# A two-block transformer kernel: prefetches and side-by-side sums between stages, a shorter VectorE tail, four store places

## The chip, the cores and the metric

One core of a Trainium2 chip runs the whole program in one launch. The metric is device time in microseconds (us). The kernel before took 3588.96 us in the median of three runs (3581.26 to 3589.14).

## The reference, cut to what matters

A sequence of 1024 tokens of width 1024 goes through two blocks, all in float32.

```
# block 1
u = rms_norm(x); proj = u @ w_in
xa = causal_conv(x_rnn); r, i = sigmoid(xa @ wa + ba), sigmoid(xa @ wx + bx)
a = exp(-8 r softplus(-lam)); b = sqrt(1 - a*a) * (i * xa); h_t = a_t h_(t-1) + b_t
ya = h * gelu(g_rnn)
yb = attention(low-rank q, low-rank k and v, per-head rms_norm, rope)
x = x + (sigmoid(g0) * ya + sigmoid(g1) * yb) @ w_out
x = x + moe(rms_norm(x))      # 32 experts, top 2 in one group
# block 2
mix = [hgrn2(x) | multiscale_pool(x)] @ w_out_2
h = layer_norm(alpha * x + mix)
out = layer_norm(alpha * h + moe_2(h) + shared(h))   # 64 experts, top 8
```

Each expert is `(silu(x @ w_gate[e]) * (x @ w_up[e])) @ w_down[e]`, with weights of 3 MB.

## The kernel before, in words

The program is a chain of stages, one function each, and each has its own block of instruction streams. When a stage ends, its semaphores are cleared and all engines meet (`phase`, the `clear` callback), so that no engine enters the next stage before every engine, SyncE (SP) and GpSimd (POOL) among them, has finished this one. The order is: `begin` (norm and turn), `lru` (recurrence of block 1), `mla_project`, `attention`, `merge`, `route1`, `dispatch`, `experts`, `take_sums`, `hgrn`, `pooling`, `mix_out`, `route2`, `dispatch`, `experts`, `final_norm`. Within a stage each engine runs its own list in program order and waits on semaphores. SP issues nearly all loads and stores; they are served in order of issue.

`lru` works in four blocks of 256 channels. For each, TensorE (PE) does three groups of input products and two gate groups, ScalarE (ACT) takes each group out of PSUM with its function, and VectorE (DVE) does the convolution and then the tail: `hh = aa*aa` (L525), `pp` (L528), `ii*xa` (L531), `ii*pp` (L534), two scans (L537), `hh*gelu` (L539), `hh*gate` (L541). After block 4 PE also does the low-rank products of token tile 0 (`low_rank`, L571). POOL clears the second copy of the rows in which experts' outputs are summed (`zero_second`, L276).

`mla_project` goes over eight tiles of 128 tokens. PE turns the tile's low-rank rows (`turn_low`, L662), does the low-rank products of the next tile (`low_groups`, L653), then the up-projections (`up_groups`, L679), and between the query and the key/value part turns the heads of the tile before (`turn_heads`, L692, eight steps). ACT copies every turned group into `stage` (`take_heads`, L762); SP stores two steps together (L637) from one of two places of `stage`, so the fifth step waits until the store of the first two has landed.

`merge` computes the two sigmoid gates' remaining half with weights `w_gate` loaded at its start (L1102), then the output product. `route1` picks experts and has SP load the weights of the first five experts (L1626, L1631). `dispatch` works out which token stands in which slot and stores the weights per token (`dense`, L1454). `experts` loops over blocks of 2 x 64 slots: POOL gathers token rows (`gather`: L1753, L1756, L1757), PE turns them (L1814), DVE copies them out (L1911 for the first block, L1902 later) and also copies the second half's weights (`stage_gate_up`, L1888), PE multiplies (L1825, L1828, L1851, L1854), POOL adds the result to `token_sums` in DRAM (L1778). The two halves of a block go to two copies of the sums.

`take_sums` adds the two copies: SP loads tile t of the first (L1247), POOL then has a DMA add the second to it (`add_second`, L1230), PE turns it (L1260), DVE copies it (L1267). `final_norm` does the same addition and then the last layer norm and the stores. `pooling` loads its weights `w`, `w_pool` and `w_out` (L2287 to L2289) while POOL clears the second copy of the sums again.

Of the kernel before, what the change touches and what calls it, by code (L numbers as in the profile page):

```python
# [18 lines left out]
F32 = mybir.dt.float32  # L19
# [253 lines left out]
def zero_second(pool, sum_d, zero, zero_out):  # L273

    for t in range(T + 1):
        pool.dma_start(sum_d[S + P + t * P:S + P + (t + 1) * P, :], zero).then_inc(zero_out, 16)  # L276


def lru(nc, A, G, spare, sum_d, wcol, wgate, w_low, ps):
# [9 lines left out]
    with ph.ctx:  # L289
# [43 lines left out]
        def _(pool):  # L333
# [6 lines left out]
            zero_second(pool, sum_d, zero[:, 0:D], zero_out)  # L340
            pool.wait_ge(zero_out, 16 * (len(spare) + T + 1))
# [48 lines left out]
        def _(a):  # L390
# [9 lines left out]
            with a.Fori(0, NBLK // 2) as j:  # L400
                for u in range(2):
# [12 lines left out]
                    for k, (out, bias) in enumerate(((rr, vec(G, "lru_ba")), (ii, vec(G, "lru_bx")))):  # L414
                        a.wait_ge(group_ready, first + 4 + k)
# [7 lines left out]
                    a.wait_ge(log_ready, b + 1)  # L423

                    s.activation(pp[:], rr[:], ACT.Tanh, scale=-1.0).then_inc(p_ready, 1)
# [5 lines left out]
        def _(v):  # L431
# [66 lines left out]
            with v.Fori(0, NBLK) as b:  # L498
# [3 lines left out]
                for k in range(CONV):  # L502
                    for c in range(B):
# [10 lines left out]
                        else:  # L514
# [3 lines left out]
                d.memset(xp[:, :, 0:CONV - 1], 0.0).then_inc(pad_ready, 1)  # L518
                v.wait_ge(group_taken, 1 + b * GROUPS + 4)
# [3 lines left out]
                                ALU.mult).then_inc(log_ready, 1)  # L523
                v.wait_ge(act, b * 3 + 3)
# [5 lines left out]
                v.wait_ge(group_taken, 1 + b * GROUPS + 5)  # L530
                st(d.tensor_tensor(ii[:], ii[:], xa[:], ALU.mult))  # L531
                st.join()
# [5 lines left out]
                st.join()  # L538
                st(d.tensor_tensor(hh[:], hh[:], gelu[:], ALU.mult))  # L539
# [36 lines left out]
def mla_project(nc, A, G, qk_d, v_d, w_low, ps):  # L576
# [12 lines left out]
    with ph.ctx:  # L589
# [9 lines left out]
        stage = ph.sb("stage", [QK, 2, 2 * TURN, P])  # L599
# [3 lines left out]
        sq_low = ph.sb("sq_low", [P, Q_LORA + KV_LORA])  # L603
        rot_all = ph.sb("rot_all", [P, 4, HEADS, H2])
        rot = [rot_all[:, i] for i in range(4)]
        acc = ps[:, 0].rearrange("p b s -> p (b s)").rearrange("p (k n) -> p k n", n=BANK)
# [4 lines left out]
         st_out1, dve, act) = ph.sems(  # L611
            "w_in1 w_in2 acc_ready acc_taken row_sq row_ms row_rt row_ok tr_ready tr_taken "
            "q_sq qk_sq qk_ms qk_rt qk_ok ht_ready ht_taken v_out st_out0 st_out1 dve act")
        st_out = [st_out0, st_out1]
# [13 lines left out]
        def _(sp):  # L628
            sp.dma_start(w_uq[:], A["w_uq"].rearrange("l (c p) n -> p (l c) n", p=P)).then_inc(w_in1, 16)
            sp.dma_start(w_ukv[:], A["w_ukv"].rearrange("l (c p) n -> p (l c) n", p=P)).then_inc(w_in2, 16)  # L630
            for t in range(T):
                sp.wait_ge(acc_taken, number["up", t, NQ + NKV - 1] + 1)
                sp.dma_start(v_d[t * P:(t + 1) * P, :], vv[:].rearrange("p h d -> p (h d)")).then_inc(v_out, 16)
                for n in range(TURNS // 2):
# [3 lines left out]
                                 stage[:, n % 2]).then_inc(st_out[n % 2], 16)  # L638
            sp.wait_ge(v_out, 16 * T)
            for q in st_out:  # L640
                sp.wait_ge(q, 16 * T * TURNS // 4)

        @block.tensor
        def _(pe):
# [60 lines left out]
        def _(a):  # L705
# [49 lines left out]
            def take_heads(t):  # L755
                for n in range(TURNS):
                    m = t * TURNS + n
                    a.wait_ge(ht_ready, m + 1)
                    d = (m // 2)
                    if n % 2 == 0 and d >= 2:  # L760
                        a.wait_ge(st_out[(n // 2) % 2], 16 * (d // 2))
                    s.activation(stage[:, (n // 2) % 2, (n % 2) * TURN:(n % 2 + 1) * TURN, :],  # L762
# [80 lines left out]
def attention(nc, A, G, qk_d, v_d, mask_d):  # L843
# [25 lines left out]
    with ph.ctx:  # L869
# [42 lines left out]
        def _(sp):  # L912
# [20 lines left out]
            for p in range(PAIRS - 2):  # L933
                reload(p)

# [125 lines left out]
def merge(nc, A, G, rows_d, sum_d, logits):  # L1061
# [5 lines left out]
    COL = 2 * D + Q_LORA + KV_LORA + ROPE + D  # L1067
    HC = C // 2
    with ph.ctx:
        w_gate = ph.sb("w_gate", [P, 2, C, D // 4])  # L1070
# [17 lines left out]
        (wg0, wg1, wo_in, x_in, g_ready, g_taken, m_ready, o_ready, o_taken, dve) = ph.sems(  # L1088
            "wg0 wg1 wo_in x_in g_ready g_taken m_ready o_ready o_taken dve")
        wg = [wg0, wg1]  # L1090
# [5 lines left out]
        def _(sp):  # L1096
            w = A["w_in"].rearrange("l (c p) n -> p (l c) n", p=P)
            for q in range(Q):
                if q >= 2:
                    sp.wait_ge(g_ready, (q - 1) * PERQ)  # L1100
                c0 = COL + q * (D // Q)
# [132 lines left out]
def take_sums(nc, G, sum_d, rows, cols):  # L1234

    ph = phase(nc)
    with ph.ctx:
# [11 lines left out]
        @block.gpsimd  # L1249
        def _(pool):  # L1250
            add_second(pool, sum_d, rows, row_in, both_in)
# [1472 lines left out]
```

## Time and profile before

| | us |
|---|---|
| median of 3 runs | 3588.96 |
| the profiled execution | 3588.82 |
| its span in the profile | 3587.1 |
| PE busy | 3219.0 (90%) |
| DVE busy | 1568.1 (44%) |
| ACT busy | 727.7 (20%) |
| POOL busy | 729.1 (20%) |

PE is busy for nine tenths of the span; the other tenth lies mostly between stages. A view of waits lists who waited for whom; a row of the timeline gives start, duration, engine and line, what is written from what, and in brackets the idle time before it and what ended it. A name such as `second` can stand for several tensors in turn, since the kernel uses two large buffers again and again.

### The profile page before, as it was taken

The page shows a single profiled execution, that of the slowest core. Times are in us where ns is not written, and L with a number is a line of the kernel's source. Part 1 is how long each engine was busy: PE and PEld are TensorE (multiplying, and loading weights), DVE is VectorE, ACT ScalarE, POOL GpSimd, SP SyncE. Part 2 cuts the span into 40 slices and gives each one's busy share as a digit, 9 for nine tenths or more (in the row PEclk, how much of TensorE's full clock was granted, in tenths as well). Part 3 has the DMA queues.
Part 4 walks back from the last instruction along what each step waited for, and adds up shares of the span by engine and source line. Part 5 has one row for each costly group of instructions (what it writes and reads, how often), then busy time and mean ns, then how long its engine had stood idle before and what let it go on. Part 6 is the DMA issues. An engine that isn't in the chain of part 4 may idle for free. (4 is left out here: it accounts for less than half of the span.)

```text
span 3587.1 us, 44543 instructions
## 1 busy us (share of the span) xinstructions
PE 3219.0 (90%) x14147; PEld 1604.3 (45%) x14148; DVE 1568.1 (44%) x2350; ACT 727.7 (20%) x1169; POOL 729.1 (20%) x932
## 2 busy tenths in 40 slices
PE   8999899978998995989779996989799999999992
PEld 4444455545664454333257773455333333333330
DVE  3332224455773123434336773334344444444444
ACT  2222123334552011011023230121011111111112
POOL 1000000000000000444410000000255555555552
PEclk9999999998999996999879998989899999999996
DMA  6110021123212115899541003111698999988876
GB/s 221 41 41 29 0 100 49 51 56 83 72 48 83 66 71 208 306 382 384 186 118 34 25 1 126 68 58 58 241 307 266 330 323 313 297 278 274 275 245 182
DMA packets 177205, 564.82 MB, mean 157 GB/s; under 512 B 18636, under 2 KB 88880, under 8 KB 139952
## 3 DMA queue, kind: packets, MB, share of 16 engines
q1 hardware_dynamic: 139456, 428.64, 31.5%
q0 software_dynamic: 35856, 133.74, 15.2%
q10 hardware_dynamic: 1800, 1.20, 0.1%
q8 instruction: 58, 0.95, 0.1%
q14 instruction: 35, 0.29, 0.0%
HBM read 460.27 MB, written 103.27 MB: 157 GB/s over the span
## 5 line engine op out<-in xcount | busy, mean ns | idle before, releaser
L1825 PE MATMUL gu_ps<-w_gu,second 128*64 x1680 | 755.5, 603 | 13.2 <-DVE h L1888 8.0
L1828 PE MATMUL gu_ps<-h,second 128*64 128x512 f32 x1680 | 755.5, 603 | 0.0
L1825 PEld LDWEIGHTS gu_ps<-w_gu,second 128*64 128x64 f32 x1680 | 224.3, 138 | 456.0 <-issue 444.1
L1753 POOL COPY idx<-moe_slot_tok 128x1 int32 (+1 forms) x109 | 22.2, 204 | 1782.4 <-POOLq L95 1739.9
L1851 PE MATMUL y_ps<-w_dn,hid_t 128*64 x824 | 375.6, 598 | 2.5 <-issue 2.2
L1854 PE MATMUL y_ps<-second,hid_t 128*64 128x512 f32 x824 | 375.6, 598 | 0.0
L352 PE MATMUL front<-second,wcol 128*128 128x512 f32 x768 | 330.4, 592 | 4.8 <-ACTq L63 2.4
L1888 DVE COPY h<-w_gu 128x4096 f32 x109 | 249.5, 2290 | 71.6 <-SPq L1705 71.3
L352 PEld LDWEIGHTS front<-second,wcol 128*128 128x128 f32 x768 | 145.8, 190 | 188.6 <-issue 188.6
L1773 POOL TENSOR_TENSOR idx_y<-moe_slot_tok,moe_side 128x1 int32<-128x1 int32 x103 | 123.4, 1198 | 522.3 <-ACT second L1874 522.3
L1828 PEld LDWEIGHTS gu_ps<-h,second 128*64 128x64 f32 x1680 | 224.3, 138 | 0.0
L1874 ACT ACTIVATE second<-y_ps,share 128x1024 f32<-128x1024 f32 x103 | 114.7, 1113 | 459.1 <-PE y_ps L1854 459.1
L1868 ACT ACTIVATE act_g<-gu_ps 128x256 f32<-128x256 f32 x105 | 40.3, 384 | 749.8 <-PE gu_ps L1828 749.8
L1851 PEld LDWEIGHTS y_ps<-w_dn,hid_t 128*64 128x64 f32 x824 | 104.3, 136 | 191.6 <-issue 180.0
L1777 POOL TENSOR_TENSOR mark_y<-tok 128x1 f32<-128x1 f32 x103 | 181.2, 1759 | 19.1 <-DMA token_sums<-second,idx_y 8.4
L1778 POOL DMA_INDIRECT token_sums<-second,idx_y x103 | 175.0, 1699 | 18.3 <-issue 17.4
L1900 DVE TENSOR_TENSOR hid<-act_g,gu_ps 128x256 f32<-128x256 f32 x105 | 44.2, 421 | 291.5 <-ACT act_g L1868 291.5
L1904 DVE COPY hid_t<-h_ps 128x256 f32<-128x256 f32 x105 | 44.5, 424 | 279.4 <-PE h_ps L1837 279.4
L1814 PEld LDWEIGHTS x_ps<-ident,xb 128*128 128x128 f32 x856 | 105.0, 195 | 108.6 <-issue 73.8
L1895 DVE COPY second<-w_dn 128x2048 f32 x105 | 129.0, 1229 | 47.1 <-issue 47.0
L1814 PE MATMUL x_ps<-ident,xb 128*128 128x128 f32 x856 | 125.8, 290 | 22.2 <-DMA xb<-token_rows,idx 21.9
L1902 DVE COPY second<-x_ps 128x1024 f32<-128x1024 f32 x105 | 128.5, 1224 | 24.5 <-PE x_ps L1814 24.5
(435 smaller groups left out, 4887.1 us busy)
## 6 DMA issues: line engine op xcount, KB each, us to landing
w_gu<-in_w_gate_dram SPq DMA_DIRECT2D x96, 1024.0 KB, 13.3
w_gu<-in_w_up_dram SPq DMA_DIRECT2D x96, 1024.0 KB, 17.3
w_dn<-in_w_down_dram SPq DMA_DIRECT2D x96, 1024.0 KB, 10.4
wcol<-in_w_in_dram SPq DMA_DIRECT2D x12, 1024.0 KB, 5.3
qk_by_head<-stage SPq DMA_DIRECT2D x32, 384.0 KB, 3.3
qk<-qk_by_head SPq DMA_DIRECT2D x16, 768.0 KB
token_sums<-zero POOLq DMA_DIRECT2D x19, 512.0 KB, 13.1
token_sums<-second SPq DMA_DIRECT2D x16, 512.0 KB, 2.6
```

Of the source, the lines that this page charges most:

```text
L352: last = nc.tensor.matmul(ps[:, slot, c, h * BANK:(h + 1) * BANK], wcol[:, k, kc, c * P:(c + 1) * P], G.u[:, kc, h * BANK:(h + 1) * BANK], ...
L1773: g.tensor_tensor(idx_y[:, slot:slot + 1], G.slot_tok[:, bass.ds(b, 1)], G.side, ALU.add).then_inc(idx_y_ready, 1)
L1777: g.tensor_tensor(mark_y[:, slot:slot + 1], G.tok[:, 0:1], G.tok[:, 0:1], ALU.add).then_inc(idx_y_ready, 1)
L1778: g.indirect_dma_start(sum_d, bass.IndirectOffsetOnAxis(ap=idx_y[:, slot:slot + 1], axis=0), y[:, slot, :], None, compute_op=ALU.add).then ...
L1814: last = nc.tensor.transpose(x_ps[:, c, :], xb[:, slot, c:D:C], G.ident[:])
L1825: nc.tensor.matmul(gu_ps[0:PART, slot], x_t[:, slot, c, 0:PART], w_gu[:, bass.ds(ws, 1), :, c, :].rearrange("p o g n -> p (o g) n"), start ...
L1828: last = nc.tensor.matmul(gu_ps[PART:P, slot], x_t[:, slot, c, PART:P], st_gu[:, slot, :, c, :], start=c == 0, stop=c == C - 1)
L1851: nc.tensor.matmul(y_ps[0:PART, cs], hid_t[:, slot, c, 0:PART], w_dn[:, bass.ds(ws, 1), c, cs].rearrange("p o n -> p (o n)"), start=c == 0 ...
L1854: last = nc.tensor.matmul(y_ps[PART:P, cs], hid_t[:, slot, c, PART:P], st_dn[:, c, cs], start=c == 0, stop=c == FC - 1)
L1888: d.tensor_copy(st_gu[:, slot].rearrange("p g c n -> p (g c n)"), w_gu[:, bass.ds(e % W, 1)].rearrange("p o g c n -> p (o g c n)")).then_i ...
L1895: d.tensor_copy(st_dn.rearrange("p c n -> p (c n)"), w_dn[:, bass.ds(e % W, 1)].rearrange("p o c n -> p (o c n)")).then_inc(d_staged, 1)
L1902: d.tensor_copy(x_t[:, 1 - slot], x_ps[:]).then_inc(x_ready, 1)
```

## The change

- `lru`, DVE: `gate*gelu` is done as soon as the gate has been taken, so one multiplication follows the scans in place of two; `ii*xa` goes ahead of `aa*aa`. ACT: `Tanh` goes between the two gate sigmoids.
- `lru`, POOL: after the first block it clears a third copy of the sums; the second expert loop and `final_norm` use that third copy, and `pooling` no longer clears anything.
- `mla_project`: `stage` has four places; `rot_all` and `sq_low` lie inside `sq`; for tile 0 `low_groups(1)` goes ahead of `turn_low(0)`.
- `attention`/`merge`: the first two parts of `w_gate` are loaded at the end of `attention`'s SP list.
- `route1` loads two experts; the other three are loaded at the head of `dispatch`'s SP list.
- `dispatch`: POOL gathers the rows of the first two blocks there (waiting for the slots and for the store of `dense`); some tiles of the first `dispatch` lie in the free large buffer. `experts` starts without these gathers, and DVE stages the weights of block 0 ahead of the copy of its rows.
- `take_sums`: ACT's queue loads the second copy by plain loads, DVE adds. `final_norm`: the same for the first two of eight tiles, the other six as before.

```diff
@@ lru
+            pool.wait_ge(block_done, 2)
+            zero_second(pool, sum_d, 2, zero[:, 0:D], zero_out)
...
+                        if k == 1:
+                            a.wait_ge(log_ready, b + 1)
+                            s.activation(pp[:], rr[:], ACT.Tanh, scale=-1.0).then_inc(p_ready, 1)
...
+                v.wait_ge(group_taken, 1 + b * GROUPS + 3)
+                st(d.tensor_tensor(gate[:], gate[:], gelu[:], ALU.mult))
...
+                v.wait_ge(group_taken, 1 + b * GROUPS + 5)
+                v.wait_ge(act, b * 3 + 2)
+                st(d.tensor_tensor(ii[:], ii[:], xa[:], ALU.mult))
                 v.wait_ge(act, b * 3 + 3)
                 st(d.tensor_tensor(hh[:], aa[:], aa[:], ALU.mult))
...
-                st(d.tensor_tensor(hh[:], hh[:], gelu[:], ALU.mult))
@@ mla_project
-        stage = ph.sb("stage", [QK, 2, 2 * TURN, P])
+        stage = ph.sb("stage", [QK, 4, 2 * TURN, P])
...
+                if t == 0:
+                    low_groups(1)
                 turn_low(t)
-                if t + 1 < T:
+                if 0 < t < T - 1:
                     low_groups(t + 1)
...
-                    if n % 2 == 0 and d >= 2:
-                        a.wait_ge(st_out[(n // 2) % 2], 16 * (d // 2))
+                    if n % 2 == 0 and t:
+                        a.wait_ge(st_out[n // 2], 16 * t)
@@ attention, sync
+            for q in range(2):
+                load_gate(sp, A, G, w_gate, q)
@@ take_sums
+        @block.scalar
+        def _(a):
+            for t in range(T):
+                at = S + P + t * P
+                a.dma_start(other[:, t, :], sum_d[at:at + P, :]).then_inc(row_in[t], 16)
...
+            for t in range(T):
+                v.wait_ge(row_in[t], 32)
+                d.tensor_tensor(rows[:, t, :], rows[:, t, :], other[:, t, :], ALU.add).then_inc(added, 1)
+                if t:
+                    take(t - 1)
+            take(T - 1)
@@ route1, sync
-            for e in range(W1):
+            for e in range(W_EARLY):
                 load_expert(sp, G, e, e)
@@ dispatch
+            if scores is None:
+                for e in range(W_EARLY, W1):
+                    load_expert(sp, G, e, e)
             sp.wait_ge(dense_ready, 1)
...
+        @block.gpsimd
+        def _(pool):
+            g = nc.gpsimd
+            pool.wait_ge(slots_ready, 1)
+            for b in range(2):
+                g.tensor_copy(G.idx[:, b:b + 1], G.slot_tok[:, b:b + 1]).then_inc(idx_ready, 1)
+            pool.wait_ge(idx_ready, 2)
+            pool.wait_ge(dense_out, 16)
+            g.tensor_tensor(G.mark[:], G.tok[:, 0:2], G.tok[:, 0:2], ALU.add).then_inc(idx_ready, 1)
+            for b in range(2):
+                g.indirect_dma_start(G.xb[:, b, :], None, rows_d, bass.IndirectOffsetOnAxis(
+                    ap=G.idx[:, b:b + 1], axis=0)).then_inc(G.xb_in[b], 16)
@@ experts
-            gather(0, 0)
-            gather(1, 1)
...
+            stage_gate_up(0, 0)
             v.wait_ge(x_turned, 1)
             d.tensor_copy(x_t[:, 0], x_ps[:]).then_inc(x_ready, 1)
-            stage_gate_up(0, 0)
             stage_gate_up(1, 1)
@@ pooling
-            nc.gpsimd.memset(zero[:], 0.0).then_inc(cleared, 1)
-            pool.wait_ge(cleared, 1)
-            zero_second(pool, sum_d, zero[:], zero_out)
-            pool.wait_ge(zero_out, 16 * (T + 1))
@@ final_norm (FIRST = 2)
+            for t in range(FIRST):
+                at = 2 * (S + P) + t * P
+                a.dma_start(other[:, t, :], sum_d[at:at + P, :]).then_inc(other_in[t], 16)
...
+            for t in range(FIRST):
+                v.wait_ge(row_in[t], 16)
+                v.wait_ge(other_in[t], 16)
+                d.tensor_tensor(G.h[:, t, :], G.h[:, t, :], other[:, t, :], ALU.add).then_inc(both_in[t], 1)
```

## Rows read from the trace of the kernel before

**Rows 1.** The page, part 1: busy us, share, instructions.

```profile
PE 3219.0 (90%) x14147; PEld 1604.3 (45%) x14148; DVE 1568.1 (44%) x2350; ACT 727.7 (20%) x1169; POOL 729.1 (20%) x932
```

**Rows 2.** Waits of PE, whole run: us in total, times, longest us.

```profile
PE tp L1260 <- DMA second<-token_sums: 35.7, 8, 29.6
...
PE x_ps L1814 <- DMA xb<-token_rows,idx: 21.9, 2, 15.0
PE u_ps L2310 <- DMA w_pool<-in_w_pool_dram: 19.9, 1, 19.9
PE front L692 <- ACT stage L762: 17.9, 22, 2.1
...
PE front L662 <- DVE low L798: 16.8, 1, 16.8
...
PE ps L1133 <- DMA w_gate<-in_w_in_dram: 8.3, 1, 8.3
```

**Rows 3.** Timeline, end of the first recurrent stage.

```profile
423.85 1.91 ACT L425 ACTIVATE pp<-rr 128x2048 f32<-128x2048 f32 x1
...
433.54 2.28 DVE L531 TENSOR_TENSOR ii<-ii,xa 128x2048 f32<-128x2048 f32 x1
...
445.13 2.29 DVE L541 TENSOR_TENSOR h<-hh,gate 128x2048 f32 x1
```

**Rows 4.** Timeline, start of the projection stage.

```profile
448.24 0.17 DVE L786 COPY gains<-vec 128x6 f32<-128x6 f32 x1 [0.82 <-PEq L95]
...
452.72 1.97 PE L662 MATMUL front<-ident,low 128*128 128x128 f32 x8 [16.82 <-DVE low L798]
...
469.41 15.61 PE L679 MATMUL front<-w_uq,low_t 128*128 128x512 f32 x36
```

**Rows 5.** DMA issues: line, count, KB each, median us to landing.

```profile
w_ukv<-in_w_ukv_dram SPq DMA_DIRECT2D x1, 2048.0 KB, 18.3
...
w_pool<-in_w_pool_dram SPq DMA_DIRECT2D x1, 256.0 KB, 17.2
...
token_rows<-dense SPq DMA_DIRECT2D x1, 128.0 KB, 21.5
```

**Rows 6.** Timeline, heads turned in tile 6 of the projection stage.

```profile
747.02 1.05 PE L692 MATMUL front<-ident,qk 128*96 128x128 f32 x8 [0.28 <-ACT stage L762]
...
750.14 1.13 PE L692 MATMUL front<-ident,qk 128*96 128x128 f32 x8 [2.07 <-ACT stage L762]
```

**Rows 7.** Timeline, start of the merge stage.

```profile
1117.28 1.02 SPq L1102 DMA_DIRECT2D w_gate<-in_w_in_dram  x2
...
1123.81 11.53 PE L1133 MATMUL ps<-second,w_gate 128*128 128x512 f32 x21 [8.35 <-DMA w_gate<-in_w_in_dram]
```

**Rows 8.** Timeline, first dispatch and start of the first expert loop.

```profile
1404.14 0.38 SPq L1454 DMA_DIRECT2D token_rows<-dense  x1
...
1430.44 1.05 POOL L1757 DMA_INDIRECT xb<-token_rows,idx  x1 [0.37 <-issue]
...
1434.90 1.98 PE L1814 MATMUL x_ps<-ident,xb 128*128 128x128 f32 x8 [6.94 <-DMA xb<-token_rows,idx]
```

**Rows 9.** Timeline, the stage that adds the two copies of the sums.

```profile
1788.67 4.16 SPq L1247 DMA_DIRECT2D second<-token_sums  x8
...
1822.23 1.09 PE L1260 MATMUL tp<-ident,second 128*128 128x128 f32 x8 [0.66 <-DMA second<-token_sums]
1823.36 1.22 DVE L1267 COPY h<-tp 128x1024 f32<-128x1024 f32 x1 [0.53 <-PE tp L1260]
```

**Rows 10.** One window of that stage: length, busy us, PEclk, DMA share, GB/s.

```profile
1791.00:1792.00 1.00, 0.00 (x0) 0.00 (x0) 0.00 (x0) 0.00 (x0) 0.00 (x0) 0.50 1.01 385
```

**Rows 11.** Timeline, start of the second expert loop.

```profile
2533.47 0.49 SPq L1631 DMA_DIRECT2D w_dn<-in_w_down_dram  x1
...
2540.80 1.97 PE L1814 MATMUL x_ps<-ident,xb 128*128 128x128 f32 x8 [14.97 <-DMA xb<-token_rows,idx]
```

**Rows 12.** Groups by line: busy us, mean ns, idle before.

```profile
L1888 DVE COPY h<-w_gu 128x4096 f32 x109 | 249.5, 2290 | 71.6 <-SPq L1705 71.3 <-issue 0.2
```

More of the change, by code:

```diff
@@ L840, in _, with attention @@
             norm_heads(T - 1)
-def attention(nc, A, G, qk_d, v_d, mask_d):
+def attention(nc, A, G, qk_d, v_d, mask_d, w_gate):
     ph = phase(nc)
@@ L1237, in take_sums @@
     with ph.ctx:
+        other = ph.sb("other", [P, T, D])
         tp = ph.ps("tp", [P, 2, C, P])
-        turned, taken = ph.sems("turned taken")
+        turned, taken, added = ph.sems("turned taken added")
         row_in = ph.sems(" ".join(f"row_in{t}" for t in range(T)))
-        both_in = ph.sems(" ".join(f"both_in{t}" for t in range(T)))
         block = ph.ctx.enter_context(nc.Block())
@@ L1255, in _ @@
             for t in range(T):
-                pe.wait_ge(both_in[t], 16)
+                pe.wait_ge(added, t + 1)
                 if t >= 2:
@@ L1406, in shared_add, with dispatch, room @@
                                    op0=ALU.mult, op1=ALU.add).then_inc(G.sh_added, 1)
-def dispatch(nc, G, K, E, NB, rows_d, sum_d, scores=None):
+def dispatch(nc, G, K, E, NB, rows_d, sum_d, n, scores=None):
     ph = phase(nc)
     with ph.ctx:
-        m = ph.sb("m", [P, T, E])[:] if scores is None else G.m
-        before = ph.sb("before", [P, T + 1, E])
-        dense = ph.sb("dense", [P, T, E])
+        taken = [0]
+        def room(name, n):
+            if scores is not None:
+                return ph.sb(name, [P, n])[:]
+            taken[0] += n
+            return G.u[:].rearrange("p c s -> p (c s)")[:, taken[0] - n:taken[0]]
+        m = room("m", T * E).rearrange("p (t e) -> p t e", e=E) if scores is None else G.m
+        before = room("before", (T + 1) * E).rearrange("p (t e) -> p t e", e=E)
+        dense = room("dense", T * E).rearrange("p (t e) -> p t e", e=E)
         cnt = ph.sb("cnt", [P, E])
@@ L1658, in experts @@
         w_gu, w_dn = G.w_gu, G.w_dn
-        idx = ph.sb("idx", [P, 2], I32)
         idx_y = ph.sb("idx_y", [P, 2], I32)
-        mark = ph.sb("mark", [P, 2])
         mark_y = ph.sb("mark_y", [P, 2])
@@ L1664, in experts @@
         share_b = ph.sb("share_b", [P, 2])
-        xb = ph.sb("xb", [P, 2, D + E])
+        xb, idx, mark = G.xb, G.idx, G.mark
         act_g = ph.sb("act_g", [P, 2, F_EXP])
@@ L1928, in moe_state @@
     G.first = sb(f"moe_first{E}", [1, E], I32)[:]
+    G.xb = sb(f"moe_xb{E}", [P, 2, D + E])
+    G.idx = sb(f"moe_idx{E}", [P, 2], I32)
+    G.mark = sb(f"moe_mark{E}", [P, 2])
+    G.xb_in = [nc.alloc_semaphore(f"xb_in{i}_{E}") for i in range(2)]
     G.used = sb(f"moe_used{E}", [1, 1], I32)[:]
@@ L2253, in _, with pooling @@
             take_out(H - 1, H)
-def pooling(nc, A, G, sum_d, w_out):
+def pooling(nc, A, G, w_out):
     ph = phase(nc)
@@ L2483, in final_norm @@
         junk = ph.sb("junk", [P, 2, D])
+        other = ph.sb("other", [P, FIRST, D])
         total = ph.sb("total", [P, T])
@@ L2672, in program @@
                 G.x2 = second[:]
-                attention(nc, A, G, qk_d, v_d, mask_d)
-                merge(nc, A, G, rows1_d, sum_d, logits[:])
+                G.gate_in = [nc.alloc_semaphore(f"gate_in{i}") for i in range(2)]
+                with nc.sbuf_tensor("w_gate", [P, 2, C, D // 4], F32) as w_gate:
+                    attention(nc, A, G, qk_d, v_d, mask_d, w_gate)
+                    merge(nc, A, G, rows1_d, sum_d, logits[:], w_gate)
             G.w_gu = moe.enter_context(nc.sbuf_tensor("w_gu_1", [P, W1, 2, C, F_EXP], F32))
@@ L2693, in program @@
             G.w_out_in = nc.alloc_semaphore("w_out_in")
-            pooling(nc, A, G, sum_d, w_out)
+            pooling(nc, A, G, w_out)
             moe_state(nc, moe, G, K2, E2)
```

110 lines of the change are left out of this document (51 added, 59 removed).

## The prediction

> **What bounds the kernel now.** The page comes first: PE is busy for 90% of the span [rows 1], so its busy time is the floor and whatever the change can give lies in PE's idle stretches. The list of PE's waits says where these are [rows 2]: 35.7 us for the summed rows, 21.9 for gathered rows at the head of the two expert loops, 19.9 for `w_pool`, 17.9 for `stage`, 16.8 for the first normed low-rank rows, 8.3 for `w_gate`. The change touches each of them. The timeline around each tells what ends last there and what would be next.
>
> **Last block of `lru`.** PE is through with its work before VectorE's tail, and all engines meet after L541, which ends at 447.42 [rows 3]. `Tanh` (1.91) leaves ACT's path to `aa`, since ACT waits for PE between the two gate groups; no table load stands ahead of it. One 2.29 multiplication moves ahead of the tail. `ii*xa` (2.28) leaves it too, but `Sqrt` (the size of `Tanh`, 1.91) then shows in its place, so 0.3 is left. Sum: 1.91 + 2.29 + 0.3 = 4.5 us. In the other blocks the tail lies beside some 80 us of PE's products and gives nothing. ACT's second gate sigmoid is now queued behind `Tanh`, which waits for DVE's scaling; if it came late, PE's next block would wait. Bounds 3.5 to 4.8.
>
> **First tile of `mla_project`.** The stage starts 0.8 after the tail, at 448.2; PE turns at 452.72 and the up-projections start at 469.41, 21.2 after the start [rows 4]. Between turn and up-projection lie 14.7 us of `low_groups(1)`. They now start at once: 14.7, up to 2 for the slow clock, the turn 1.0, then DVE's copy of 1.22, which nothing covers any more: 18.9. The floor behind it is the load of `w_ukv`, landing 18.3 after its issue at +0.4, at 18.7 [rows 5]. Gain 2.2 (0 to 3).
>
> **Four store places.** Of the 22 waits for `stage` seven, one for each of tiles 0 to 6, are of 2.0 us, and 15 of 0.26 (7 x 2.0 + 15 x 0.26 = 17.9) [rows 2]. The pattern is that of tile 6: 0.28 before the fifth step, 2.07 before the seventh, since ACT's fifth copy waits for a store [rows 6]. With four places the store waited for is a tile old, and the short handshake stays: 7 x (2.0 - 0.26) = 12.2 us. `rot_all` and `sq_low` share memory with `sq`, but no wait is added and the old order keeps them apart: ACT squares anew only after the heads were turned. Bounds 10 to 15.
>
> **`w_gate` ahead.** The merge stage starts at 1117.28, the first product at 1123.81 [rows 7]. The two loads are now last in attention's SP list, behind value reloads needed two head pairs before the end, so nothing is queued behind them and some 60 us are left to land. Gain 1123.8 - 1117.4 = 6.4 us (5.5 to 9). `w_out` moves 1 us ahead and is needed 120 us later.
>
> **Routing, first dispatch, first expert loop.** With six loads in place of fifteen `route1` no longer ends with SP's issuing, and `dispatch` starts several us earlier. That buys nothing directly: `dense` is stored behind the same 15.7 MB, lands at 1404.14 + 21.5 = 1425.6 [rows 5, 8], and POOL waits for exactly that. From there: mark and issue 0.6, so 1426.2 where it was 1430.44; landing 4.46 later (1434.90 - 1430.44), at 1430.7; the turn 1.98, ending at 1432.7; the copy 1.22. DVE's 2.29 copy of the weights [rows 12] now runs while the gather lands: POOL's second issue ends at 1428.3, the stage starts 0.9 later, weights are staged by 1431.9. First product at 1433.9 where the same sum gives 1434.90 + 1.98 + 1.22 + 2.29 = 1440.4; a handshake of some 0.4 falls away: 6.9 us (0 to 8). This loop waits 71.3 us for weights (L1705) [rows 12], but their stream stands still until PE frees the first slot, so it moves forward with PE.
>
> **`take_sums`.** From 1788.67 to 1824.6 [rows 9]. Now sixteen plain loads of 512 KB, 8.39 MB. One queue's plain loads moved 385 GB/s at full DMA share [rows 10]: 21.8 us, 1.4 until bytes flow, so 1811.9. Behind the last: DVE's addition (a row of this kind and size, 1.22), PE's turn 1.1 to 2.0, the copy 1.22: 1816.4. Gain 8.0. The far bound is the stage's own mean while accumulating, 8.39 MB in 33.5 us: then the last landing stays where it is and the addition comes on top, 2 us lost; the near one is 9.5.
>
> The Trainium skill (DMA: Bandwidth & Descriptors, "Anatomy of one DMA — SWDGE (gpsimd) path") fits a DMA issued by GpSimd as 2.0 us plus its bytes at 436 GB/s. By that, an estimate for queues it wasn't fitted on, the loads would take 21.2 us and the gain be 10.
>
> **`pooling`.** `w_pool` lands 17.2 after its issue [rows 5], with `w` (2.1 MB) ahead of it and POOL's 4.7 MB of zeros beside both. Alone, 2.36 MB at 385 GB/s are 6.1, with 2.0 fixed: 8.1. Gain 9.0 (5 to 10). The zeros go into `lru` after its first block, beside weights that are asked for a group or more ahead, each 0.5 of POOL's time, and PE has there no wait on a DMA: nothing. If that cover failed, one late group would cost a few us.
>
> **Second expert loop.** The rows are gathered while the shared expert runs, 40 us before use. What is next: SP issues six loads (to 2533.96) [rows 11] before it passes on that expert 0 has landed; then DVE's 2.29, then the row copy 1.22: product at 2537.7. Before: 2540.80 + 1.97 + 1.22 + 2.29 and gaps, 2546.7. Gain 9.0 (6 to 9.5). PE is the bound in this loop, so the shift lasts.
>
> **`final_norm`.** A plain load of 512 KB is 1.36 us of all DMA engines (at 385 GB/s); an accumulating one is (33.5 - 8 x 1.36) / 8 = 2.8 [rows 9, 10]. DMAs set the pace there, so two exchanges give 2 x (2.8 - 1.36) = 2.9; DVE's two additions stand before the first norm, while it waits. Bounds 0 to 5.
>
> **Sum.** 4.5 + 2.2 + 12.2 + 6.4 + 6.9 + 8.0 + 9.0 + 9.0 + 2.9 = 61.1 us. The profiled execution took 3588.82 (span 3587.1 and 1.7 around it), 0.1 below the median of the runs: 3588.8 - 61 = 3528 us. With all low bounds 3560, with all high ones 3514.
>
> **Rivals.**
> - A, plain loads crawl too: two queues of rows from DRAM run at the mean of the accumulating stage. `take_sums` loses 2 in place of winning 8, `final_norm` wins nothing: 3528 + 10 + 3 = 3541. For it: the DMA share is full in that stage. Against: 385 GB/s at the same share before the additions [rows 10].
> - B, the store wait only moves: stores queue behind each other and the next tile waits. All 12.2 lost: 3540. Against: four stores in some 31 us of tile time.
> - C, weights bound the first expert loop whatever PE's start: 6.9 lost, 3535. For it the 71.3 us [rows 12]; against it the stream's halt named above.
> - D, the merge stage starts at the full clock. Its first 21 products took 11.53 after 8.35 idle [rows 7], at full rate 21 x 0.434 (15.61 / 36 [rows 4]) = 9.1. With a stop of 1.9 us in place of 8.35, 2.4 more could fall away: 3526. The Trainium skill (TensorE: Matmul & The Clock Gate, "Part 1: The HAM clock gate") says that PE falls to half rate when it has been idle and not after a brief stop. I don't count it: the granted clock can also fall some time after PE has resumed.
> - E, slower: one step of the expert loops gets longer. `xb`, `idx` and `mark` lie elsewhere and the second loop adds into the third copy; GpSimd handles each of 109 blocks. From 61 / 109 = 0.56 us a block the whole gain is gone; at 0.7 it is 3604. For it: PE has no slack in the second loop. Against: the instructions are the same, and PE waits for gathered rows only twice, at the two starts [rows 2].
>
> **How the numbers follow.** The forecast as summed 0.60 (3518 to 3538), A 0.12, B 0.07, C 0.09, D 0.09, E 0.03. 3514 to 3545 holds all but E and the outermost of A with B. A change of 0.3% (11 us) is about what a measurement of this kernel can tell from none; only E, or half of the terms failing at once, ends there: faster 0.95, same 0.02, slower 0.03.
>
> **What would show it.** `w_gate`, `w_pool` and `xb` gone from, or small in, PE's waits; `stage` near 5.5; one multiplication behind the scans and `Tanh` between the sigmoids; `take_sums` some 28 us long with its last load about 23 after its start; first product of the second loop some 7 after the stage's start. I am wrong if the loops' blocks lengthen, if `dense` lands later than 42 us after routing starts, or if the plain loads stay under 300 GB/s.

## The result, and the profile after

The changed kernel took 3526.1 us (median of four runs, 3521.2 to 3527.8) where the kernel before took 3588.4 beside it: a ratio of 0.983 with a 95% interval of 0.981 to 0.985. The forecast was 3528. The profiled execution took 3527.6 with a span of 3525.9, 61.2 us less than the span before. PE does the same work with less idle time; part 1 of the page, as in [rows 1]:

```profile
PE 3216.6 (91%) x14147; PEld 1603.9 (45%) x14148; DVE 1579.0 (45%) x2360; ACT 728.2 (21%) x1169; POOL 714.7 (20%) x919
```

PE's waits over the whole run (us in total, times, longest). `w_gate` is gone from the list, `stage` is down to the short handshakes, and where the two expert loops waited for gathered rows there is now a wait of 17.9 for PE's own queue (PEq) at a stage's start (answers to [rows 2]):

```profile
PE tp L1274 <- DVE second L1287: 27.6, 8, 22.3
...
PE x_ps L1859 <- PEq L95: 17.9, 2, 12.9
...
PE u_ps L2351 <- DMA w_pool<-in_w_pool_dram: 11.2, 1, 11.2
...
PE front L696 <- ACT stage L768: 5.5, 21, 0.3
```

Every stretch below is read off the two timelines, between the first rows of stages or to a first product (us). Together they make up the whole 61.2.

| stretch | before | after | gained | forecast |
|---|---|---|---|---|
| last low-rank products of `lru` to the next stage | 26.7 | 22.3 | 4.4 | 4.5 |
| projection stage, start to first up-projection | 21.2 | 19.9 | 1.3 | 2.2 |
| from there to the merge stage | 647.9 | 633.8 | 14.0 | 12.2 |
| merge stage | 265.8 | 256.8 | 9.0 | 6.4 |
| routing to first product of the first expert loop | 57.8 | 56.0 | 1.8 | 6.9 |
| from there to `take_sums` | 347.8 | 348.8 | -1.0 | 0 |
| `take_sums` | 36.7 | 27.7 | 9.0 | 8.0 |
| pooling, start to first product | 17.8 | 9.1 | 8.7 | 9.0 |
| second expert loop, start to first product | 15.9 | 7.1 | 8.7 | 9.0 |
| from there to `final_norm` | 988.3 | 984.7 | 3.6 | 0 |
| `final_norm` | 52.1 | 49.8 | 2.2 | 2.9 |
| all the rest | | | -0.5 | 0 |

The timeline of the tail of `lru` (answers to [rows 3]; columns here and below: start, us, engine, line). One multiplication stands behind the scans, and the next stage starts at 444.9:

```profile
419.90 1.91 ACT L420 ACTIVATE pp<-rr 128x2048 f32<-128x2048 f32 x1 [1.70 <-DVE rr L527]
...
441.84 2.29 DVE L544 TENSOR_TENSOR h<-hh,gate 128x2048 f32 x1
```

PE at the start of the projection stage (to [rows 4]). The 48 low-rank products now start at once, but take 17.35 where the same 48 take 14.37 in the later tiles, since the granted clock was 0.50 (1.2 GHz) until about 451. The load of `w_ukv` landed 18.6 after the stage's start and was not what PE waited for last. In two later runs with the same code here (`e_dense1` and `e_both1`) the clock was back by 449, the first up-projection came 18.9 and 19.0 after the start, and PE's last wait ahead of it was for `w_ukv`: that is the floor that the prediction named.

```profile
445.10 17.35 PE L657 MATMUL front<-w_low,second 128*128 128x384 f32 x48 [8.11 <-PEq L95]
...
464.85 15.69 PE L683 MATMUL front<-w_uq,low_t 128*128 128x512 f32 x36 [1.52 <-ACT low L728]
```

The merge stage (to [rows 7]): the first product stands 0.04 behind the stage's start. The windows (length, PE busy with count, granted clock, DMA share, GB/s) show that the clock was not lowered there:

```profile
1098.68 0.37 SPq L1115 DMA_DIRECT2D w_out<-in_w_out_dram  x1
...
1098.72 1.53 PE L1144 MATMUL ps<-second,w_gate 128*128 128x512 f32 x3 [1.46 <-PEq L95]
```

```profile
1098.00:1102.00 4.00, 3.27 (x8) 1.00 0.51 160
1102.00:1106.00 4.00, 4.00 (x10) 1.00 1.03 415
```

The first dispatch and the start of the first expert loop (to [rows 8]). Read three gaps: `dense` stored at 1372.60 and awaited until 1398.3; the gathers issued by 1401.37; and then nothing on any engine until PE turns rows at 1406.75, without waiting for them. The trace has the landing of the second gather at 1405.69:

```profile
1372.60 3.14 SPq L1489 DMA_DIRECT2D token_rows<-h  x1
...
1398.30 0.19 POOL L1506 TENSOR_TENSOR moe_mark<-tok 128x2 f32<-128x2 f32 x1 [3.39 <-DMA token_rows<-h]
...
1400.41 0.96 POOL L1508 DMA_INDIRECT moe_xb<-token_rows,moe_idx  x1 [0.30 <-issue]
...
1406.75 1.95 PE L1859 MATMUL x_ps<-ident,moe_xb 128*128 128x128 f32 x8 [12.94 <-PEq L95]
1407.77 2.29 DVE L1933 COPY h<-w_gu 128x4096 f32 x1 [13.22 <-SPq L1751]
...
1411.52 1.11 PE L1870 MATMUL gu_ps<-w_gu,second 128*64 x1 [2.82 <-DVE second L1957]
```

`take_sums` (to [rows 9]), and two of its windows (to [rows 10]). A pair of rows comes in about every 2.6 us from 1765 on, at over 400 GB/s:

```profile
1760.31 4.22 ACTq L1265 DMA_DIRECT2D other<-token_sums  x8
...
1765.20 1.23 DVE L1287 TENSOR_TENSOR second<-second,other 128x1024 f32<-128x1024 f32 x1 [16.45 <-DMA other<-token_sums]
...
1786.07 1.22 DVE L1283 COPY h<-tp 128x1024 f32<-128x1024 f32 x1 [0.62 <-PE tp L1274]
```

```profile
1768.00:1772.00 4.00, 2.67 (x12) 0.50 1.03 421
...
1780.00:1784.00 4.00, 3.37 (x15) 0.50 0.59 231
```

The start of the second expert loop (to [rows 11]). The turn is over at 2486.4, but VectorE's copy of the weights waits for SP, which first issues six loads:

```profile
2484.49 1.95 PE L1859 MATMUL x_ps<-ident,moe_xb 128*128 128x128 f32 x8 [4.99 <-PEq L95]
...
2486.93 0.46 SPq L1679 DMA_DIRECT2D w_dn<-in_w_down_dram  x1
2487.67 2.30 DVE L1933 COPY h<-w_gu 128x4096 f32 x1 [6.91 <-SPq L1751]
...
2491.41 1.11 PE L1870 MATMUL gu_ps<-w_gu,second 128*64 x1 [4.97 <-DVE second L1957]
```

### The profile page after: what moved, and what is told of

Read it like the earlier page. It is cut to its first block and busy times, and to the rows that moved or that the text cites. A ratio compares the mean times of both kernels' runs of the same rounds, so it can differ in the third digit from the quotient of the medians.

```text
span 3525.9 us, 44548 instructions
## 1 busy us (share of the span) xinstructions
PE 3216.6 (91%) x14147; PEld 1603.9 (45%) x14148; DVE 1579.0 (45%) x2360; ACT 728.2 (21%) x1169; POOL 714.7 (20%) x919
## 5 line engine op out<-in xcount | busy, mean ns | idle before, releaser
L1859 PEld LDWEIGHTS x_ps<-ident,moe_xb 128*128 128x128 f32 x856 | 104.4, 193 | 105.0 <-issue 94.3
L1859 PE MATMUL x_ps<-ident,moe_xb 128*128 128x128 f32 x856 | 125.1, 290 | 18.7 <-PEq L95 17.9
```

The costliest lines, as they stand in the source:

```text
L1859: last = nc.tensor.transpose(x_ps[:, c, :], xb[:, slot, c:D:C], G.ident[:])
```

## The experiments

Each kernel is the changed one with one edit, or several where the text says so; the diffs are shortened. Times are medians, with the ratio to the kernel before on the same chip and its interval where there is one; single terms are read from the stages in their profiles, since executions of one kernel lie up to 12 us apart.

### Where the first dispatch's gain went

**Gathers back at the start of the expert stage.**

```diff
 dispatch, GpSimd:  -  indirect_dma_start(G.xb[:, b, :], ...)   # b = 0, 1, first dispatch only
 experts, GpSimd:   +  the same two, ahead of everything else, where W == W1
```

> The changed kernel, but the two gathers of the first dispatch are issued again at the start of the first expert loop; their indices and mark stay in the dispatch. Question: what became of the 6.9 us forecast for the first expert loop, of which 1.8 came. In the changed kernel the second gather is issued at 1400.4, the expert stage starts at 1406.4 and its first product comes at 1411.5. Theory (a stage's end waits until GpSimd's gathers have landed): without gathers outstanding the stage starts 0.9 after dense has landed (1398.0), so at 1399 on that clock, the rows land 5 later, turn 2.0, copy 1.2: first product at 1407.6, 3.9 us earlier. Rival (another engine holds the stage's end, and the gathers only happen to be there): the stage still starts at 1406.4, the gathers land 5 later and the first product comes at 1415, 3.5 us later than in the changed kernel.

3520.3 us in two runs (0.981, 0.979 to 0.983). Timeline:

```profile
1398.93 2.87 POOL L1434 DMA_INDIRECT moe_xb<-token_rows,moe_idx  x1 [1.55 <-POOLq L95]
1399.38 2.29 DVE L1940 COPY h<-w_gu 128x4096 f32 x1 [6.01 <-SPq L1756]
...
1405.29 1.97 PE L1866 MATMUL x_ps<-ident,moe_xb 128*128 128x128 f32 x8 [12.64 <-DMA moe_xb<-token_rows,moe_idx]
...
1408.85 1.11 PE L1877 MATMUL gu_ps<-w_gu,second 128*64 x1 [1.59 <-DVE second L1964]
```

VectorE is in the new stage 45.0 us after routing began (1354.34), where it was 52.3 in the changed kernel. So no other engine held the stage's end, and the rival falls. The gain is smaller than the theory said: routing to first product 54.5 us, against 55.6 to 56.7 in eight profiles with gathers and store as in the changed kernel (in the ninth, `e_late2` below, routing itself was 2.7 longer and it was 58.0). That is 1 to 2 us in place of 3.9. The missing part is in the first row: the gather waits 1.55 as the stage begins and then takes 2.87 to issue, where it took 1.04 inside the dispatch.

The second row points to where the 2.87 come from. VectorE's copy of the weights, which the change put at the stage's start, begins 0.45 behind the gather and is over at 1401.67; the gather's issue is over at 1401.80. Of the 1526 gathers in all fourteen profiles 66 took 2.4 to 3.1 us to issue: each of them overlaps such a copy and ends 0.1 or 0.9 behind the copy's end. The other 1460 took 1.1 or less, and at most their last 0.4 has a copy beside it. So what goes with a slow issue is a copy of the weights beside it, not being first; no run took the copy away from this gather to prove it.

**Dense stored ahead of the nine loads.**

```diff
 dispatch, SP:
+   sp.wait_ge(dense_ready, 1); store of dense
    for e in range(W_EARLY, W1): load_expert(sp, G, e, e)
-   sp.wait_ge(dense_ready, 1); store of dense
```

> The changed kernel with the store of dense ahead of the nine weight loads in SP's list of the first dispatch. Theory (the store lands late because it queues behind 15.7 MB of weights): it now lands behind 6.3 MB, some 10 us after its issue in place of 25.4, the indices (ready at 1394.6) become the bound, the gathers go out 3.5 us earlier, and so does the first product of the expert loop: 3.5 us less. If the stage's end waits for the gathers' landing, the stage starts some 6 us behind the first gather's issue again. Rival (weights bound the first expert loop whatever its start): the first product comes earlier, and the loop's first waits for weights grow by the same 3.5 us.

3523.8 us in two runs (0.982, 0.980 to 0.984).

```profile
1397.96 0.18 DVE L1662 CAST moe_slot_tok<-empty 128x32 int32<-128x32 f32 x1
1399.08 1.04 POOL L1508 DMA_INDIRECT moe_xb<-token_rows,moe_idx  x1 [0.29 <-issue]
1400.42 0.95 POOL L1508 DMA_INDIRECT moe_xb<-token_rows,moe_idx  x1 [0.30 <-issue]
1406.59 1.94 PE L1859 MATMUL x_ps<-ident,moe_xb 128*128 128x128 f32 x8 [9.17 <-PEq L95]
```

GpSimd waits for `dense` no more; the indices are its bound. Routing to first product is 52.2, some 3.4 to 4.5 less, as the theory said. The loop behind it (342.9) gave nothing back. PE's turn again comes 5.2 behind the end of the second issue (1401.37), and 1.07 behind its landing (1405.52).

**Both.**

> Both edits of the first dispatch together: dense stored ahead of the nine loads, gathers issued at the start of the expert stage. Theory: the dispatch ends with VectorE (1394.6), the stage starts at 1395.4, rows land 5 to 6 later, turn 2.0 and copy 1.2: first product at 1404.6 where the changed kernel had 1411.5, so 6.9 us less in all, about 3519. Rival (something other than gathers and dense holds the stage's end): less than 3 us. Rival (weights bound the loop): the loop gives back what its start wins.

3522.3 us in four runs, 3514.9 to 3525.2 (0.982, 0.981 to 0.984). Routing to first product 51.2, 4.4 to 5.5 less than the changed arrangement; the other 2 of the 6.9 are the slow first gather again (1.55 and 2.87, with VectorE's copy beside it, as above). The loop took 342.9 here too.

**Gathers outstanding at another stage's end.**

```diff
 dispatch, GpSimd, second dispatch only:
+   pool.wait_ge(sum_out, 16 * T)      # ahead of the mark and the two gathers
```

> The changed kernel, but in the second dispatch GpSimd issues its two gathers only when the last summed rows are stored, so that they are outstanding when that stage ends. Theory (a stage's end waits for the gathers' landing): the second expert stage starts 6 to 7 us later after the last product of the shared expert than in the changed kernel (where it is 4.9), with its turn at once behind its start. Rival (a stage's end waits only until they are issued): the stage starts about 3 us later, and the turn waits some 3 us for the rows.

3528.8 us (one run).

```profile
2477.67 1.03 POOL L1510 DMA_INDIRECT moe_xb<-token_rows,moe_idx  x1 [0.51 <-issue]
2479.01 0.94 POOL L1510 DMA_INDIRECT moe_xb<-token_rows,moe_idx  x1 [0.30 <-issue]
2485.26 0.33 SPq L1676 DMA_DIRECT2D w_gu<-in_w_gate_dram  x1
2485.46 1.95 PE L1861 MATMUL x_ps<-ident,moe_xb 128*128 128x128 f32 x8 [12.53 <-PEq L95]
```

From the store of `dense` to the stage's start 101.9 us in place of 94.4, and PE's wait ahead of the turn 12.5 in place of 5.0, so 7.5 later (6 to 7 were expected). PE's turn, the stage's first product, comes 5.5 after the second issue has ended (5.4 in the first dispatch of the changed kernel), and PE has no wait for rows left. The rival, an end that waits for the issue alone, said 3 and a wait for the rows. So a stage in which GpSimd has gathers outstanding ends only when they have landed. The traces' own landing times bear that out: there are eleven such stage ends in ten profiles, the next stage's first product comes 5.1 to 5.5 behind the end of the second issue, and 1.06 or 1.07 behind its landing in nine of them, 1.16 and 1.22 in the other two. What in the stage's end waits for the landing, the profile doesn't show.

### One part undone at a time

**Two store places.**

```diff
-   stage = ph.sb("stage", [QK, 4, 2 * TURN, P])
+   stage = ph.sb("stage", [QK, 2, 2 * TURN, P])     # and two semaphores, as before
```

> The changed kernel with two store places for the turned heads in place of four, all else kept. Theory (the wait is gone, not moved): seven waits of 2.0 us for stage come back in place of 0.26, 12.2 us, in tiles 0 to 6 ahead of the seventh step, and with them the half clock behind the first of them, some 1.4 more: the stage is 12 to 14 us longer, about 3539 in all. Rival (the gain came with the clock or from the shared memory of sq): less than 8 us longer with the waits back, or longer waits than before at other steps.

3542.1 us in three runs (0.987, 0.985 to 0.989), 16 more than the changed kernel. Projection to merge takes 669.9 where the changed kernel took 653.8. The waits are back in the same places (first row; the second is the seventh step of tile 0):

```profile
PE front L696 <- ACT stage L769: 17.7, 21, 2.1
```

```profile
522.26 1.12 PE L696 MATMUL front<-ident,qk 128*96 128x128 f32 x8 [2.00 <-ACT stage L769]
...
526.07 5.42 PE L683 MATMUL front<-w_ukv,low_t 128*128 128x512 f32 x12 [0.97 <-ACT qk L745]
```

They are 12.2 us of the 16.1, as the theory says; 12 to 14 in all were expected. With them came a wait of 1.0 for ACT (second row). In the two tiles behind it the clock was lowered just after the wait: sixteen up-projections took 8.73 in place of 7.03 (granted 0.58 from 569 to 573), and one tile later the eighth step took 1.94 in place of 1.13 and the up-projections 7.87 (0.57 from 613 to 617). Less 0.2 at the stage's start, that makes up the 16.1 to within 0.3.

**`w_gate` loaded in the merge stage.**

```diff
 attention, SP:  -  for q in range(2): load_gate(sp, A, G, w_gate, q)
 merge, SP:      +  load_gate for q = 0 and 1 at the start
```

> The changed kernel with the first two loads of w_gate back at the start of the merge stage. From there to routing the changed kernel took 256.8 us and the kernel before 265.8. Theory D (the earlier start also keeps TensorE at its full clock): the first product comes 6.5 us after the stage's start, at half clock for some 5 us, and the stage is 9 us longer, of which 2.4 are clock. Rival (the clock would have been the same and the load alone counts): 6.4 us longer. In both about 3535 or 3533; the granted clock of the first 8 us and the length of the stage tell.

3529.7 us in three runs, 3526.6 to 3538.5 (0.984, 0.982 to 0.987).

```profile
1100.05 1.02 SPq L1070 DMA_DIRECT2D w_gate<-in_w_in_dram  x2
...
1106.78 5.49 PE L1141 MATMUL ps<-second,w_gate 128*128 128x512 f32 x6 [8.14 <-DMA w_gate<-in_w_in_dram]
```

```profile
1108.00:1112.00 4.00, 4.00 (x6) 0.50 1.03 409
1112.00:1114.00 2.00, 2.00 (x6) 0.92 1.02 408
```

The stage is 264.8 long against 256.8. The first product waits 6.7, and the first 48 took 23.6 where 48 at full rate (0.434 each, as in the prediction) are 20.8: 2.8. Some 1.5 of these 9.5 come back later, since behind the gate products (1223) the clock stayed at 1.00 in this run, where it fell to 0.54 and 0.61 in the changed kernel (1212 to 1216). Theory D holds for the stage: the idle start brings the half clock with it. The medians of the whole kernel are only 3.6 apart, since the runs spread over 12 us; the 8.0 are read from the stage.

But an early load does not make the full clock certain. In eleven of the twelve profiles with `w_gate` loaded ahead the first 48 products took 20.8. In `e_dense1` they took 22.3: there the clock fell to 0.50 at about 1097, still in attention and behind a stop of 1.82, and was back only at 1103, 3 us into the products.

**Adding loads in `take_sums`.**

```diff
-   ACT: plain loads of other; DVE: rows += other
+   GpSimd: add_second(pool, sum_d, 1, 0, rows, row_in, both_in)
```

> The changed kernel with take_sums as before: eight plain loads and eight adding ones on GpSimd's queue, no addition on VectorE. The changed stage took 27.7 us. Theory (an adding load costs 2.8 us of all DMA engines where a plain one costs 1.36): the stage is 36 to 37 us long again, 9 us more, about 3535. Rival (half of the gain came from elsewhere, such as a chip's own memory speed in that profile): less than 5 us more.

3534.5 us in three runs (0.985, 0.983 to 0.987). The stage is 36.3 long, where it is 27.7 to 29.5 in all profiles with plain loads: 7 to 9 us, as the theory says.

**Zeros at the start of pooling.**

```diff
 lru, GpSimd:      -  pool.wait_ge(block_done, 2); zero_second(pool, sum_d, 2, ...)
 pooling, GpSimd:  +  memset; zero_second(pool, sum_d, 2, ...)
```

> The changed kernel with the nine zero stores back at the start of the pooling stage, and none of them in the recurrent stage. Theory (they delayed w and w_pool, and cost nothing in the recurrent stage): the first product of pooling comes 17.8 us after the stage's start in place of 9.1, 8.7 us more, about 3535; the recurrent stage is as long as with them. Rival (the zeros cost part of it in the recurrent stage): that stage gets shorter by over 0.5 us.

3534.9 us in three runs (0.985, 0.983 to 0.987).

```profile
2134.65 4.89 POOL L277 DMA_DIRECT2D token_sums<-zero  x9 [0.30 <-POOL zero L2327]
2150.40 2.05 PE L2357 MATMUL u_ps<-h,w 128*128 128x512 f32 x2 [19.14 <-DMA w_pool<-in_w_pool_dram]
```

First product 17.0 after the stage's start (9.1 without the zeros), the stage 92.6 long against 83.4. That is 7.9 and 9.2, around the 8.7 expected. The projection stage starts at 443.95; in the runs that clear in `lru` it started between 443.9 and 445.2, so the zeros cost nothing there.

**Old order in the first tile.**

```diff
-   if t == 0: low_groups(1)
    turn_low(t)
-   if 0 < t < T - 1: low_groups(t + 1)
+   if t < T - 1: low_groups(t + 1)
```

> The changed kernel with the order of the first tile of the projection stage as it was: TensorE turns tile 0 before the second tile's low-rank products. From the stage's start to the first up-projection the changed kernel takes 19.9 us and the kernel before took 21.2. Forecast for the move was 2.2. Theory (the move pays only because TensorE need not wait idle, and most of it is eaten by low-rank products at half clock): with the old order 21.2 again, 1.3 us more. Rival (w_ukv's landing sets both): 19.9 in both orders.

3527.0 us (one run).

```profile
449.59 1.97 PE L666 MATMUL front<-ident,low 128*128 128x128 f32 x8 [12.44 <-DVE low L801]
451.35 16.06 PE L657 MATMUL front<-w_low,second 128*128 128x384 f32 x48
```

The up-projections start 22.2 after the stage, not 21.2: here the 48 products lost more to half clock (16.06 in all) than in the kernel before (15.09 from 454.48 on). Both guesses miss. The old order took 21.2 and 22.2 in its two profiles, the new one 18.9 to 20.1 in twelve, so the order is worth 1 to 3 us, and how long the clock stays low decides where in that range.

### The last stage, and a kernel with all of it

**Four and eight rows added on VectorE.**

```diff
-   FIRST = 2, all additions ahead of the first norm
+   FIRST = 4 (8);  add(0); add(1); in the loop over t, behind negate(t + 1): add(t + 2)
```

> The changed kernel with four summed rows of the last stage loaded plainly and added on VectorE in place of two, each addition two rows ahead of its norm and not all in front. The changed stage takes 49.8 us (48.9 to 49.8 in the runs so far). Theory (adding loads, 2.8 against 1.36 of all DMA engines, pace the stage): two more exchanges give 2.9 us, and VectorE, at 4.4 us a row where it adds, is not yet the bound: 46 to 47. Rival (the stores of the output and the norms of each row pace it): 49, no gain.

> The same with all eight rows loaded plainly, no adding load left in the last stage. Theory: all rows are in 23 us after the stage's start and VectorE is the bound, 8 rows at 4.4 us from 5.5 us on and the last store 3 us behind: 44 us, 5 to 6 less than the changed kernel. Rival (the norms at 3.8 us a row pace it anyway, and the additions on VectorE come on top of them): 50 or more.

Four rows: 3525.5 us (one run), and the stage takes 45.0, 4 to 5 less than the 49.0 to 49.8 of the changed arrangement. Eight rows: 3532.1 us (one run), and the stage takes 56.6, longer than before the change. The row that decides when the first norm starts, first of four rows, then of eight:

```profile
3497.39 1.28 DVE L2604 SCALAR_TENSOR_TENSOR second<-second,total,gain 128x1024 f32<-128x1024 f32 x1 [6.86 <-DMA bias<-in_ln_b_dram]
```

```profile
3499.49 1.28 DVE L2604 SCALAR_TENSOR_TENSOR second<-second,total,gain 128x1024 f32<-128x1024 f32 x1 [13.63 <-DMA bias<-in_ln_b_dram]
```

`gain` and `bias` stand behind the plain rows in ACT's list, and each is written 512 KB wide; the first norm waits for them. In the changed kernel it waited 2.25. For eight rows the rival had the right size and part of the cause. The stage is 11.6 longer than with four: 7.1 of it because the first norm starts later (25.7 after the stage's start, not 18.6), which nobody expected, and 4.5 from there to the last row, since five additions of 1.2 stand between the norms in place of one, as the rival said.

**All that the runs point to.** Beside both edits of the dispatch and `FIRST = 4`:

```diff
 experts, SP:     +  landed_gate_up(0, 32)                # ahead of the loads, not behind them
 final_norm, ACT: +  gain, bias right behind other[0]     # in place of behind the last other
```

> The changed kernel with what the runs point to: in the first dispatch dense stored ahead of the nine loads and the gathers issued at the start of the expert stage (6.6 us between routing and the first product against the run of the same job with the old order); in the second expert loop SP passes on that expert 0 has landed before it issues its six loads (VectorE's copy of 2.3 us then starts with the stage in place of 3.4 us later: 3 us); in the last stage four rows added on VectorE, each two rows ahead, and gain and bias loaded right behind the first row (VectorE waited 6.9 us for bias in the run with four rows and 13.6 in that with eight, where they were loaded last: stage 40 us in place of 49.8). Together some 19 us less than the changed kernel, about 3507; ratio to the kernel before 0.977. If the vectors' load delays the rows by what it saves, the last stage stays at 45 and the time is 3512.

3516.2 us in five runs, 3510.9 to 3521.6 (0.980, 0.979 to 0.982), 10 less than the changed kernel and 9 more than expected, 4 more than in the worse case that was allowed for. The gains in the profile are 4.8 (routing to first product, 51.2), 2.5 (second loop to first product, 4.6) and 4.0 (last stage, 45.8); they make up the 11.4 us between the two spans. The last stage is where the expectation failed:

```profile
3469.66 0.47 ACTq L2566 DMA_DIRECT2D bias<-in_ln_b_dram  x1
...
3482.59 1.22 DVE L2599 TENSOR_TENSOR second<-second,other 128x1024 f32<-128x1024 f32 x1 [7.76 <-DMA other<-token_sums]
```

The vectors no longer come late, but the second row now does. In ACT's list the first row landed at 3473.50, `gain` at 3477.35, `bias` at 3479.93 and the second row at 3482.49: each vector takes a place of 2.6 to 3.9 us, since SP's rows flow beside them. What was a wait for `bias` is a wait for `other`, and with 45.8 the stage is no shorter than with four rows alone (45.0). Loading the two vectors in the stage before was not tried. The first term was expected at 6.6 and came at 4.8, which is what the 56.0 of the changed kernel and the 51.2 of the run with both edits give.

## Why the prediction was right, and where not

**The total came out closer than its terms, and that is luck.** It was 3528 against 3526.1, but of the eleven stretches one missed by 5.1 us and three went the other way by 1.8, 2.6 and 3.6. The 3.6 lie in a loop that was to gain nothing, and the 2.6 are a rival's. (The upper bounds also add up to 73.8, so the low end of the sum is 3515, not 3514; nothing hangs on it.)

**The step that failed: "the stage starts 0.9 later"** than the end of GpSimd's second issue. The stage's first product came 5.4 later, and 1.06 after the rows had landed; `e_late2` shows 5.5 and 1.06 at another place. What stands before it was right: `dense` was awaited until 42.8 us after routing began (forecast 42.5), and the gathers went out 43.6 after (43.1). I had moved two gathers to the end of a stage and counted their issue as their whole cost; the stage's end collected their landing, VectorE's copy of the weights was pushed behind it, and 1.8 us were left of 6.9.

**Rival D came true** and got 0.09: 9.0 in the merge stage, which it put at 8.8. I had refused it because the clock can also fall after PE has resumed. It did so elsewhere in these profiles, and in `e_dense1` here too (1.4 of the 2.4 lost), but in no other of the twelve profiles with the early load; and `u_gate` brings the half clock back with the load. The Trainium skill (TensorE: Matmul & The Clock Gate, "Part 1: The HAM clock gate") stood on D's side, and the rows of the changed kernel and of `u_gate` agree with it: stop of 1.46 and clock 1.00, stop of 8.14 and clock 0.50. Those of `e_dense1` don't: its clock fell to 0.50 with no longer stop than 1.82 just before.

**The clock elsewhere.** It is nearly all of the excess in the projection stage too. Of the 14.0, 12.4 are the waits for `stage` (17.9 to 5.5). Of the rest 1.5 are one place behind the first of these waits (granted 0.83 and 0.75 from 525 to 533), where the eighth step took 1.94 and sixteen up-projections 7.69, and now take 1.13 and 7.03. At the stage's start it took some of the 2.2: the products that moved ahead run at half clock, which was allowed for with up to 2 and cost 3.0. In `lru` the first block lost 1.7 (granted 0.64 and 0.51 from 34 to 38, which the profile before doesn't have); over the thirteen profiles with the changed `lru` code the same products took 83.8 in six and 82.1 in seven, as before, so this is no effect of the change.

**Right as summed:** the tail (4.4 for 4.5), the pooling stage (8.7 for 9.0; its fixed 2.0 stood in no row, but `w_pool` landed 8.5 after its issue, forecast 8.1), the second loop's start, where SP's six loads were named as the next bound (8.7 for 9.0), and `take_sums` (9.0 for 8.0). Its bytes flowed until about 1782.4 (0.59 of the window 1780 to 1784), 22.1 after the start, and its last load landed 22.8 after it, where the sum had 23.2. The estimate by the Trainium skill (DMA: Bandwidth & Descriptors, "Anatomy of one DMA — SWDGE (gpsimd) path") was 21.2; the trace lies between the two.

**Rivals that fell.** A: plain loads moved over 400 GB/s. B: the waits for `stage` are down to 5.5 and none took their place. C: with a start up to 4.8 us earlier the loop took one of the two lengths that it has anyway (below). E: a block of the second loop takes 12.12 us (median) between two starts of ACT's step, 12.13 before.

**What nobody forecast.** The second loop was 3.6 shorter from its first product on. It took 983.9 to 986.1 in all thirteen profiles of later kernels and 988.3 in the one before, where three of 80 blocks lasted 12.5, 12.6 and 13.9. `e_dense1` has such a block too (13.7), so this is most likely that one execution and no part of the change; there is no second profile of the kernel before to show it. The first loop takes either 343 to 345 or 347 to 349 with the same code, early start or late. Over all fourteen profiles the step to its 23rd block lasts 19.8 to 20.1 (eight, the long ones) or 12.7 to 14.3 (six), and that to its 15th 20.1 to 20.5 or 22.1 to 22.3. These are waits for weights. Why they come late in some executions is open.

## What to carry to other kernels

A gather moved to the end of a stage is not hidden by being issued: look whether the stage's end waits for it, and put it either well ahead of the end or behind the next start. At a start, look what VectorE does beside it: here a copy of the weights stretched its issue from 1.0 to 2.9 us. When a stall at a stage's start is taken away, count the slow clock behind it as part of the stall, and name what the first useful instruction waits for next, down to the order of issues on one queue; here that order was worth 3.4 to 4.5 us (`dense` behind nine loads) and 2.5 (a landed signal behind six), while `bias` ahead of the rows in place of behind them only moved the wait. And check a sum by its stages: a total that fits within 2 us held one term that was off by 5.

## What was not expected of the hardware

- Behind GpSimd's last gather of a stage the next stage's first product came 5.1 to 5.5 us after the issue had ended and 1.06 to 1.22 after the gather had landed, at eleven stage ends in ten profiles; with no gather outstanding the projection stage's first product came 1.0 after VectorE's last row.
- A gather whose issue overlapped VectorE's 2.3 us copy of the weights took 2.4 to 3.1 us to issue and ended 0.1 or 0.9 behind that copy, 66 times out of 66; without one (or with one in its last 0.4 only) it took 1.1 at most. The gather that begins a stage also waited 1.55 first (three profiles of three).
- A vector of 4 KB spread over 128 partitions is a transfer of 512 KB: `gain` and `bias` landed 8 and 10 us after their issue with few rows ahead, 20 and 21 with eight.
- The granted clock fell to 0.50 for some 3 to 7 us in one execution and not in another of the same work (34 to 38 in the changed kernel, 1097 to 1103 in `e_dense1`), at a cost of 1.4 to 1.7 us each time.
